# Expert retrieval in a two-layer backbone: u rows gathered by slot, v rows gathered by token, sums by 32-column strips

## The reference

```python
# per block of 128 tokens, 8 heads, 16 experts of 16384 for each head
q = (hb @ w_q).reshape(P, PEER_HEADS, 2, PEER_DKEY // 2)
s = jnp.einsum('phcd,hcnd->phcn', q, subkeys)
top_v, top_i = lax.top_k(s, PEER_TOPK)
...
expert = i1 * PEER_KEYS + i2
g = jax.nn.softmax(best, axis=-1)
a = jax.nn.gelu(jnp.einsum('pd,phkd->phk', hb, u_tab[expert]))
w = g * a
return jnp.einsum('phk,phkd->pd', w, v_tab[expert])
```

## Time and profile before

| | us |
|---|---|
| median of 2 runs | 3287.0 (3280.4 and 3293.7) |
| span of the profiled execution | 3266.4 |
| expert part of layer 0 (553 to 2190) | 1637 |
| expert part of layer 1 (2509 to 3262) | 753 |

### The profile page before, as it was taken

One profiled execution on the slowest core, in us unless ns is written; L12 is line 12 of the kernel. 1 busy time (PEld: TensorE's weight loads), 2 busy tenths in 40 slices (PEclk: granted clock), 3 DMA queues, 4 the chain that ended last, 5 costly groups with the idle time before them and its releaser, 6 DMA issues.

```text
span 3266.4 us, 28972 instructions
## 1 busy us (share of the span) xinstructions
PE 2565.1 (79%) x7008; PEld 1194.0 (37%) x7008; DVE 1877.7 (57%) x4701; ACT 802.3 (25%) x1377; POOL 988.2 (30%) x1180
## 2 busy tenths in 40 slices
PE   8998998888778878776666767679788888777666
PEld 3444644334333333332222222225466444222222
DVE  1133524888865555556666666651454788766665
ACT  2133412111112222222222222212442111122221
POOL 1000001234443333334344344321001445544433
PEclk9998879999889999998898898899889999888889
DMA  6132013799898989887898798872005999988887
GB/s 240 64 135 98 1 39 120 295 356 357 335 376 348 386 343 378 351 343 323 346 379 342 321 379 340 340 291 78 26 1 196 368 375 377 393 362 330 346 352 321
DMA packets 126146, 910.30 MB, mean 279 GB/s; under 512 B 14032, under 2 KB 15312, under 8 KB 15568
## 3 DMA queue, kind: packets, MB, share of 16 engines
q0 software_dynamic: 110592, 805.36, 60.9%
q1 hardware_dynamic: 14000, 94.30, 7.6%
q10 hardware_dynamic: 1440, 9.32, 0.7%
HBM read 907.86 MB, written 1.05 MB: 278 GB/s over the span
## 4 chain that ended last, share of the span: by engine, by line
PE 35%; DVE 23%; issue 20%; DMA 12%; ACT 5%; POOL 2%; DVEq 1%; ACTq 1%; POOLq 0%; SPq 0%; PEldq 0%
DMA regA<-uv_dram,stage 12%; PE bank L1443 10%; DVE regA L1032 9%; PE bank L1192 4%; PE bank L1119 4%; PE bank L1390 3%; DVE sqreg L1039 2%; PE bank L1156 2%; ACT mlaw L702 1%; PE bank L1202 1%; PE bank L1312 1%; PE bank L1292 1%; PE bank L1409 1%; PE bank L1133 1%; PE bank L1348 1%
## 5 line engine op out<-in xcount | busy, mean ns | idle before, releaser
L1443 PE MATMUL bank<-regA,sqreg 128*128 128x512 f32 x3072 | 1521.8, 648 | 567.8 <-DVE sqreg L1039 565.9
L1443 PEld LDWEIGHTS bank<-regA,sqreg 128*128 128x128 f32 x3072 | 609.8, 206 | 1464.0 <-DVE sqreg L1039 789.6
L1032 DVE SCALAR_TENSOR_TENSOR regA<-regA,regB 128x1024 f32<-128x1024 f32 x768 | 921.1, 1222 | 110.1 <-DMA regA<-uv_dram,stage 89.0
L373 POOL DMA_INDIRECT regA<-uv_dram,stage x768 | 842.9, 1097 | 440.3 <-POOL stage L367 310.0
L367 POOL COPY stage<-idx 128x2 int32 x384 | 122.8, 320 | 1682.7 <-PE bank L1443 938.0
L1039 DVE TENSOR_SCALAR sqreg<-con,mlaw,sqreg 128x128 f32<-128x128 f32 x768 | 236.2, 358 | 613.1 <-ACT mlaw L702 606.7
L702 ACT ACT_TABLE_LOAD x276 | 354.1, 1283 | 896.7 <-DVE regA L1032 896.4
L702 ACT ACTIVATE mlaw<-mlaw x384 | 78.1, 203 | 537.0 <-DVE regA L1032 533.9
L1409 PE MATMUL bank<-hT,wring 128*128 128x512 f32 (+1 forms) x512 | 173.3, 495 | 11.0 <-ACT hT L679 11.0
L1192 PE MATMUL bank<-hT,wring 128*128 128x512 f32 (+2 forms) x384 | 148.5, 545 | 12.9 <-ACT hT L414 9.9
L1409 PEld LDWEIGHTS bank<-hT,wring 128*128 128x128 f32 x512 | 99.1, 195 | 84.2 <-issue 76.9
(11 more groups left out here) (200 smaller groups left out, 1918.9 us busy)
## 6 DMA issues: line engine op xcount, KB each, us to landing
wring<-w_dram SPq DMA_DIRECT2D x88, 1024.0 KB, 6.7
regA<-uv_dram,stage POOLq DMA_INDIRECT x768, 9.0
mlaw<-uq_dram ACTq DMA_DIRECT2D x2, 1152.0 KB, 5.8
xT<-x_dram ACTq DMA_DIRECT2D x1, 2048.0 KB, 12.0
mlaw<-ukv_dram ACTq DMA_DIRECT2D x2, 1024.0 KB, 8.4
subk<-sk_dram ACTq DMA_DIRECT2D x2, 1024.0 KB, 4.9
out_dram<-xT SPq DMA_DIRECT2D x1, 1024.0 KB, 4.8
con<-con_dram SPq DMA_DIRECT2D x1, 937.0 KB, 4.7
```

Of the source, the lines that this page charges most:

```text
L373: g.indirect_dma_start(ring[:, s, :], None, uv_tabs[l], bass.IndirectOffsetOnAxis(stage[:, s:s + 1], 0)).then_inc(landed[s], 16)
L1032: v.scalar_tensor_tensor(out=ring[:, s, 0:D], in0=ring[:, s, 0:D], scalar=1.0, in1=hrow[:, tiles[l][n], :], op0=ALU.mult, op1=ALU.mult, ac ...
L1443: mm = p.matmul(acc[:, f * 512:f * 512 + 512], diag[:, s % DIAGS, :], ring[:, s, D + f * 512:D + f * 512 + 512], start=False, stop=False, ...
```

## The change

u and v become two tables of 4 KB rows, and each is gathered by itself. `RING` is 12 slots of 4 KB per partition.

- **u** is gathered by slot as before: one slot of 128 tokens, token on the partition, index straight from `idx`. DVE's dot (`dots`) frees the ring slot.
- The numbers of the chosen experts are also written as float32 (`eid`), PE turns them, and ACT writes them to `idxT`, in which a column is a token and the partitions are its 128 slots.
- **v** is gathered by token: the 128 rows of one token's slots, slot on the partition.
- The gelu is made once per tile on all 128 columns; DVE multiplies by the gates once (`gated`); PE turns the 128 x 128 result (`weights_turn`) and ACT writes it to the `corners` of `spread`, which POOL sets to zero once per layer. `spread[:, t, :]` is a strip of 32 columns that is zero but for one column, the token's 128 weights.
- PE (`values`) multiplies the strip by the token's gathered rows, two matmuls of 128 x 32 by 512 columns. The strip's 32 outputs are a quarter of the partitions of `acc`; token after token goes to another quarter, and each quarter accumulates over its 32 tokens.
- POOL's order: u of tile 0 alone; then u of tile i and v of tile i-1 in turn; then v of the last tile alone.
- `top_keys` runs a tile at a time, one head ahead. In layer 0 the context stream comes first, and queries are made for each stream apart (256 columns), so the 8 weight tiles of the queries are read twice. The second tile of a stream reads its key scores from a copy in SBUF (`keysB`).
- The adaLN products of layer 1 move to the phase of the last u tile of layer 0. The exponentials and the gate sums are made once per tile.

```diff
-RING = 8
-GROUP = 2
-DIAGS = 4
+RING = 12
+QUAD = 32
+QUADS = P // QUAD
+TILES = ([2, 3, 0, 1], [0, 1])
+STREAMS = ([1, 0], [0])
...
+def gather_at(l, kind, i, k):
+    base = 2 * P * FIRST[l]
+    if kind == "u":
+        return base + (k if i == 0 else P + (i - 1) * 2 * P + 2 * k)
+    if i == len(TILES[l]) - 1:
+        return base + P + i * 2 * P + k
+    return base + P + i * 2 * P + 2 * k + 1
...
-                        g.wait_ge(v_used, it * RING + (at + GROUP * (f + 1)))
-                        g.tensor_copy(stage[:, f * GROUP:(f + 1) * GROUP],
-                                      idx[:, tile % 2, bass.ds(it * RING + (h * PTOP + f * GROUP), GROUP)]).then_inc(staged, 1)
...
-                            g.indirect_dma_start(ring[:, s, :], None, uv_tabs[l],
-                                                 bass.IndirectOffsetOnAxis(stage[:, s:s + 1], 0)).then_inc(landed[s], 16)
+            def slot_free(at):
+                if at >= RING:
+                    kind, l, i, k = order[at - RING]
+                    used = dotted if kind == "u" else v_used
+                    g.wait_ge(used.sem, used.at(l, i * P + k + 1))
...
+                g.indirect_dma_start(ring[:, s, :], None, u_tabs[l],
+                                     bass.IndirectOffsetOnAxis(idx[:, i % 2, k:k + 1], 0)).then_inc(landed[s], 16)
...
+                token = k % QUADS * QUAD + k // QUADS
...
+                g.indirect_dma_start(ring[:, s, :], None, v_tabs[l],
+                                     bass.IndirectOffsetOnAxis(idxT[:, i % 2, token:token + 1], 0)).then_inc(landed[s], 16)
+                g.wait_ge(x_mid.sem, x_mid.at(l, KC))
+                g.memset(spread[:, :, :], 0.0).then_inc(cleared.sem, 1)
+                for i in range(nt + 1):
+                    for k in range(P):
+                        if i < nt:
+                            gather_u(l, i, k)
+                        if i:
+                            gather_v(l, i - 1, k)
...
+                def gelus(i):
+                    a.wait_ge(dotted.sem, dotted.at(l, (i + 1) * SLOTS))
+                    a.activation(gact, araw[:, i % 2, :], ACT.Gelu).then_inc(gelu_ready.sem, 1)
+                def weights(i):
+                    a.wait_ge(coef_mm.sem, coef_mm.at(l, i + 1))
...
+                    a.activation(corners, bank45[:, 0:P].rearrange("p (j c) -> p j c", j=QUADS), ACT.Copy).then_inc(spread_ready.sem, 1)
...
+                def dots(i, k0, k1):
+                    for k in range(k0, k1):
+                        at = gather_at(l, "u", i, k)
+                        s = at % RING
+                        v.wait_ge(landed[s], 16 * (at // RING + 1))
+                        v.scalar_tensor_tensor(out=ring[:, s, :], in0=ring[:, s, :], scalar=1.0, in1=hrow[:, i % 2, :],
+                                               op0=ALU.mult, op1=ALU.mult, accum_out=araw[:, i % 2, k:k + 1]).then_inc(dotted.sem, 1)
+                def gated(i):
+                    v.wait_ge(gelu_ready.sem, gelu_ready.at(l, i + 1))
+                    v.tensor_tensor(coef, gact, wts[:, i % 2, :], ALU.mult).then_inc(coef_ready.sem, 1)
...
+                        if i < nt and nxt[0] < nt:
+                            top_keys(*nxt, 0)
+                            top_keys(*nxt, 1)
+                        if h == 0 and i:
+                            gated(i - 1)
+                        if i < nt:
...
+                            dots(i, h * PTOP, h * PTOP + 4)
+                            if nxt[0] < nt:
+                                choose(*nxt)
+                            dots(i, h * PTOP + 4, (h + 1) * PTOP)
...
+                def both_keys(sx, q):
+                    n = (sx * HC + q) // 2
+                    p.wait_ge(pq_ready.sem, pq_ready.at(l, 2 * n + 2))
...
+                        p.wait_ge(top_done.sem, top_done.at(l, 2 * sx * PH + q // 2 if q else (2 * sx - 1) * PH))
...
+                def values(i, k0, k1):
...
+                    for k in range(k0, k1):
+                        at = gather_at(l, "v", i, k)
+                        s = at % RING
+                        j, c = k % QUADS, k // QUADS
+                        p.wait_ge(landed[s], 16 * (at // RING + 1))
                         for f in range(2):
-                            mm = p.matmul(acc[:, f * 512:f * 512 + 512], diag[:, s % DIAGS, :], ring[:, s, D + f * 512:D + f * 512 + 512],
-                                          start=False, stop=False, skip_group_check=True)
-                        mm.then_inc(v_used, 1)
+                            mm = p.matmul(acc[QUAD * j:QUAD * j + QUAD, f * 512:f * 512 + 512], spread[:, QUAD * j + c, :],
+                                          ring[:, s, f * 512:f * 512 + 512], start=(c == 0), stop=(c == QUAD - 1), skip_group_check=True)
+                        mm.then_inc(v_used.sem, 1)
```

More of the change, by code:

```diff
@@ L695, in _ @@
-                nt = len(tiles[l])
-                def gelus(n, h, g0, g1):
-                    at = ((n if l == 0 else 4 + n) * PH + h) * PTOP
-                    with a.Fori(g0, g1) as i:
-                        a.wait_ge(dotted, i * GROUP + (at + GROUP))
-                        a.activation(gact[:, bass.ds(i * GROUP + h * PTOP, GROUP)], araw[:, bass.ds(i * GROUP + h * PTOP, GROUP)],
-                                     ACT.Gelu).then_inc(gelu_ready, 1)
-                query(0)
-                query(1)
@@ new lines, in sums_out, with both @@
+                def sums_out(i):
+                    a.wait_ge(v_used.sem, v_used.at(l, (i + 1) * P))
+                    if i:
+                        a.wait_ge(yt_mm.sem, yt_mm.at(l, 2 * i))
+                    a.activation(yrow, acc[:, :], ACT.Copy).then_inc(y_ready.sem, 1)
+                def both(sx, q):
+                    query(sx, q)
+                    query(sx, q + 1)
+                both(0, 0)
+                both_keys(0, 0)
+                rows_in(0)
+                both(0, 2)
@@ L1447, in _ @@
-                query(0)
-                query(1)
-                key_scores(0)
-                key_scores(1)
-                for j in range(2 * len(tiles[l])):
-                    t, f = j // 2, j % 2
-                    if j < 2:
-                        p.wait_ge(x_mid.sem, x_mid.at(l, KC))
-                        p.wait_ge(h_ready.sem, h_ready.at(l, 2 * KC))
-                    else:
-                        p.wait_ge(hr_ready.sem, hr_ready.at(l, j - 1))
-                    for k in range(4):
-                        mm = p.transpose(ps[4 + j % 2][:, k * P:(k + 1) * P], hT[:, 4 * f + k, t * P:(t + 1) * P], ident)
-                    mm.then_inc(hr_mm.sem, 1)
```

511 lines of the change are left out of this document (275 added, 236 removed).

## The result

| | before | after |
|---|---|---|
| median, two runs each | 3287.0 us | 3167.5 us (3166.9 and 3168.2) |
| ratio | 1 | 0.965, interval 0.958 to 0.973 |
| span of the profiled execution | 3266.4 | 3165.1 |
| layer 0, first gather to the last sum | 1637 | 1530 |
| layer 1, the same | 753 | 769 |

The kernel got faster by 3.5%. Thirteen later runs of before had their median at 3273.2, so the two runs of 3287 lay some 14 us high. Against 3273.2 the changed kernel (3168.2 there) gains 105 us, and between the two profiled executions it is 101. The forecast was 54 less, 3233. Its direction held.

What follows compares the result with a forecast made beforehand. A ring of dependences (gather, dot, gelu, diagonal, sum) was taken as the bound, DMA nearest ceiling. Layers 1559 + 782 less 5 = 2336 against 2390; 3266 to 3212, plus 21: 3233 us, own range 3190 to 3275, 8-in-10 range 3130 to 3390.

Steps and rivals of the forecast that it cites:

- phases A: First tile's u gathered alone, once per layer: DVE sets the pace, 8 x 28.2 plus 6, 232 us each.
- The phase with the adaLN tiles: Third pair phase of layer 0, with 24 adaLN tiles: DMA 403 us, PE 301, taken as 410.
- The offset from the profiled execution to the median: Whole kernel: the median of the runs lies 21 us above the profiled execution, 3212 becoming 3233.
- a gain in layer 0 and a loss in layer 1: Expert tiles by layer: layer 0 1559 us against 1637, layer 1 782 against 753.
- C: Last tile's v gathered alone, once per layer: DMA sets 1.35 us a token, 183 us with chains.
- POOL's price of a pair: One u and one v gather: 2 x (1.10 + 0.30) = 2.80 us; pair taken as 2.87, 367 us a phase.
- rival 1: Pair phases: the DMA engines are the only bound, 2.66 us a pair, 3145 in all; 24 in 100.
- Rival 2: Pair phases: gathers held by dots make POOL the bound, 3.3 us a pair, 3418 in all; 16 in 100.
- Rival 3: v-alone phases: column strips run one after the other, 229 us twice, 3325 in all; 17 in 100.
- The rule on weight loads: v-alone phases: each token's four loads stand in the open, 2.55 us a token, 3540 in all; 3 in 100.
- The step on the strips: v-alone phases, PE: matmuls in different column strips overlap, 0.86 us or less per token against 1.71 without.
- DMA about half: Sign for the u-alone phases: DMA engines about half busy, with DVE over 90% and 226 to 240 us.

Runs made afterwards that it cites:

- d1: The kernel before with the gelu of two slots replaced by a plain copy: 3128.7 us against before's 3269.7.
- e1: The kernel before with ACT's hardware loop over the gelus written out, real gelu kept: 3149.3 us against before's 3272.4.
- c3: The changed kernel with each dot replaced by a plain sum over the slot, product with h left out: 3059.7 us, ratio 0.937.
- d3: The changed kernel with dots over the first 512 of 1024 columns: 2984.0 us, ratio 0.913.
- e2: The changed kernel with h left in PSUM and read there by the dots, queries using one bank: 3078.4 us, ratio 0.941.
- c1: The changed kernel with consecutive tokens put in the same strip of 32 columns: 3281.8 us, ratio 1.004.
- c2: The changed kernel with PE alternating record by record between the strips of two tokens: 3169.9 us, ratio 0.969.
- c0: The changed kernel, unedited, timed and profiled once more: 3168.2 us, ratio 0.968.

## Why the prediction was right and where it was wrong

**What failed.** The mechanism held, and the forecast of 3233 lay 65 us over the measured 3168 because three terms of its sum were mis-sized. The two phases A were priced at 232 us each and took 220 and 219 (25 us together). The phase with the adaLN tiles was priced at 410 us and took 387 (23 us). The offset from the profiled execution to the median was taken as 21 us and was 2 (19 us). What each got wrong is told below.

**Right: the loop was the bound, and cutting it pays.** d1 and e1 put 141 and 123 us on ACT's stay in before's loop. Forecasting a gain in layer 0 and a loss in layer 1 also held (1530 against 1637, 769 against 753). Its reason for layer 1, two phases that leave the DMA engines idle, holds for A alone (315 GB/s); C moved 385. ACT's table loads at the gelus fell to the 6 foreseen.

**Right, in part by luck: POOL's price of a pair.** 2.80 from 2 x (1.10 + 0.30), taken as 2.87, gave 367 for each plain pair phase. Measured were 366, 368 and 373. The means of 1.10 to 1.15 us a gather are near the 1.10 foreseen. The 0.07 on top was meant for two resources that cannot both be kept full. In the first phase and in layer 1's it was more hold instead: 2 x (1.12 + 0.30) = 2.84 and 2 x (1.15 + 0.30) = 2.90, with POOL full. Only in the second did POOL have some 10 us to spare. c3, d3 and e2 show the cause: with gathers held little or not at all, a plain pair costs 2.56 to 2.71 us (the dearer ones carry the second stream's query tiles). So rival 1 was false for this kernel, and only because dots hold gathers; freed of that it comes true and about at its own price of 2.66. Rival 2's mechanism is real, at 1.12 us a gather and not at the 1.30 from which it decides.

**Right: the strips run together, and no rule of weight loads.** Rival 3 needed 229 us for phase C and was seen only where I put neighbours into one strip (c1). The rule on weight loads would give 2.55 us a token; measured are 1.28, with four loads of 0.11 us each and none in the open. The step on the strips took an overlap too wide: 0.86 us or less. It is one neighbour in four, 1.28, which by luck equals DMA's pace. The bound by DMA came out right, as c2 shows, with PE just at it. POOL is as close: in the last three quarters of each C phase it issues a gather every 1.24 us, its own pace, and the ring hides that they land at 1.28.

**Wrong: two times of phase A (25 us).** The pace was right: dots ran from 549.0 to 774.9, 226 us for 8 heads of 28.2, and the next tile's first dot came at 780.7, 232 us after the first. But the next phase's gathers start at 764.3, under A's last dots. I counted the 6 us to the first landing and the border as an addition, then gave the next phase its full 367. The lines of this border are

```profile
764.31 1.18 POOL L407 DMA_INDIRECT regA<-u_dram,idx  x1 [2.06 <-DVE regA L1118]
774.91 1.29 DVE L1118 SCALAR_TENSOR_TENSOR regA<-regA,regB 128x1024 f32<-128x1024 f32 x1
780.74 1.22 DVE L1118 SCALAR_TENSOR_TENSOR regA<-regA,regB 128x1024 f32<-128x1024 f32 x1
```

Phases that overlap at their borders must be measured at one point; at the gathers, A is 220 and 219. The sign "DMA about half" for this phase was wrong too: its rows have 335 and 315 GB/s, some eight tenths of the fullest phase's.

**Wrong: the adaLN phase (23 us).** The term was 341 for the half gathers, 24 x 2.6 for the tiles and 7 on top, 410. At 410 GB/s (the slices of the profile page within this phase have 407 to 411, the phase's row 404), a half gather of 0.524 MB costs 1.28 us and a tile 2.56: 256 x 1.28 + 24 x 2.56 = 389. Measured: 387. So 13 of the 23 us are the 0.05 us that I put on each half gather: 0.02 from the queue's share and 0.03 on trust for smaller packets. The rest is the margin. Queue 0 of the changed kernel reads

```profile
q0 software_dynamic: 221184, 805.40, 66.9%
```

which by the same working gives 0.669 x 3165 / 1536 = 1.38 us, while the phase itself ran at 1.28. My reading is that the share counts a packet from start to end, also while it stands beside others, and so overstates the price with 12 slots in flight. A share of 1.01 in the fullest phase fits that; no run tests it. Here the GB/s of the fullest stretch was the better price.

**Small ones.** Layer 1's pair phase was 6 us longer than said, C once 7 longer (190) and once 6 shorter (177), the first gather 9 us earlier in place of 5 (in c0's profile of the same kernel only 4, so this term is scatter in part). The terms add up: -25, -23, +6, +1 and -4 are -45, with rounding -46, and -54 - 46 is the -100 between the profiled executions (101 measured).

**Wrong: the offset of 21 us.** The forecast carried the distance from the profiled execution to the median of two runs over to the changed kernel. Before's medians of 13, 12 and 6 runs were 3273.2, 3269.7 and 3272.4, so it was mostly scatter. Of the 65 us between 3233 and 3168 it is 19.

**Not priced in the prediction: the ring's depth.** I took the 12 slots for hidden cover of chains. At 8 slots the change is worth 0 us, at 12 it is 105, and with h in PSUM 14 slots give another 15 by the medians, 9 of them in the experts' phases. And I read "two gelus (0.20 plus a table load of 1.28 in most)" without asking why the load was there. One line of the program removes it, for about as much as the restructuring gives (123 and 105 us).

**Open.** The written-out loop was not tried together with h in PSUM in before's own scheme, nor late diagonals with a deeper ring. What in a gather waits for the dot is not shown, and the mean hold, 0.1 to 0.2 us in pairs and 0.4 in phase A, is read from the traces and not modelled. e1 and the changed kernel were not timed in one batch; by their ratios to before, 0.963 (0.959 to 0.968) and 0.968 (0.965 to 0.971), their order is likely and not certain.

## What to carry to other kernels

When a loop of dependences sets the pace, list each step of its round trip and ask why it is there before restructuring: a table load repeated in each turn cost 123 us here and one written-out loop removed it. Beside indirect gathers, keep DVE's long instructions to one SBUF operand, the other in PSUM (90 us). When gathers get smaller, the number in flight must grow in turn (105 us). Matmuls share the array by strips of columns only where neighbours in program order differ in their strip, so order them that way (113 us).

## What the runs showed of the hardware

- An indirect gather of 128 rows costs POOL 0.94 us and 0.30 to the next, with rows of 4 KB as with rows of 8 KB. One issued just after a dot with two SBUF operands began took up to 1.99 us and ended 0.81 us after the dot; beside a dot of the same length with one SBUF operand the mean is 0.94.
- Float32 matmuls of 128 x 32 by 512 columns: 0.43 us from start to start within one strip; about 0.03 us when the one before is in another strip (0.01 to 0.03 in c2, where every second record changes the strip). Eight records alternating between two strips take 2.33 us.
- 16 DMA engines moved 404 GB/s for 387 us in gathers of 0.5 MB and tiles of 1 MB together. A 4 KB packet took 159 ns in the median, 164 to 185 in the mean of a phase.
- ACT's table load stands in every turn of a hardware loop that is entered with another table: 276 loads against 48 for the same 384 gelus.
